# The levels of a blocked triangular inverse: one matrix at a time, or two side by side

## The reference

```python
kb = k * beta[..., None]
lower = jnp.where(strict, jnp.einsum('bnhik,bnhjk->bnhij', kb, k) * decay, 0.0)
tri = lower + jnp.eye(CHUNK, dtype=jnp.float32)
rhs = jnp.concatenate([vb, kb * jnp.exp(g)[..., None]], axis=-1)
sol = lax.linalg.triangular_solve(tri, rhs, left_side=True, lower=True)
...
def step(S, inp):
    u_i, w_i, a_i, qg_i, kt_i, gl_i = inp
    v_new = u_i - jnp.einsum('bhck,bhkv->bhcv', w_i, S)
    o_i = jnp.einsum('bhck,bhkv->bhcv', qg_i, S) + jnp.einsum('bhij,bhjv->bhiv', a_i, v_new)
    S = S * gl_i[..., None, None] + jnp.einsum('bhck,bhcv->bhkv', kt_i, v_new)
```

## Time and profile before

| | |
|---|---|
| median of 3 runs | 1374.46 us (1374.28 to 1375.1) |
| span of the profiled execution | 1372.5 us |
| PE busy | 1327.3 us, 97% of the span |
| weight loads (PEld) busy | 1076.1 us, 78% |
| DVE busy | 972.7 us, 71% |
| ACT busy | 675.3 us, 49% |
| POOL busy | 554.9 us, 40% |
| granted TensorE clock, mean | 0.995 |

### The profile page before, as it was taken

The page is one execution under the profiler, slowest core; times in us unless marked ns, Lnnn a source line. Parts: engine busy times, 40 slices in busy tenths (PEclk is TensorE's granted clock), DMA queues, the critical chain, the costliest instruction groups (busy, mean ns, idle before and its releaser), DMA issues.

```text
span 1372.5 us, 18983 instructions
## 1 busy us (share of the span) xinstructions
PE 1327.3 (97%) x7213; PEld 1076.1 (78%) x7213; DVE 972.7 (71%) x1687; ACT 675.3 (49%) x1018; POOL 554.9 (40%) x372
## 2 busy tenths in 40 slices
PE   7998999999999999999998999999999999998997
PEld 5786888888888888887886678777777878776786
DVE  5587788879787979876337856777767677777413
ACT  6354436363635445364226555556555655655203
POOL 6432334333334333332224785636365563622300
PEclk9999999999999999999999999999999999999999
DMA  7210110111102120206213211112221111119403
GB/s 195 79 36 16 31 47 16 47 47 47 47 17 62 31 62 20 61 22 223 81 43 127 89 31 31 47 47 65 66 55 47 46 47 47 46 46 306 170 1 123
DMA packets 106859, 91.46 MB, mean 67 GB/s; under 512 B 3105, under 2 KB 92306, under 8 KB 106770
## 3 DMA queue, kind: packets, MB, share of 16 engines
q1 hardware_dynamic: 106770, 90.25, 21.7%
HBM read 66.65 MB, written 23.59 MB: 66 GB/s over the span
## 4 chain that ended last, share of the span: by engine, by line
PE 80%; DVE 12%; ACT 4%; issue 3%; DMA 0%; POOL 0%; DVEq 0%; SPq 0%; ACTq 0%
PE psum L518 25%; PE psum L673 17%; PE psum L687 5%; PE psum L2462 4%; PE psum L2436 4%; PE psum L2381 2%; PE psum L2449 2%; DVE terms L1871 2%; PE psum L2369 2%; PE psum L535 2%; PE psum L2347 2%; DVE stick L2019 2%; PE psum L646 2%; PE psum L2322 1%; DVE small_L L1856 1%
## 5 line engine op out<-in xcount | busy, mean ns | idle before, releaser
L518 PE MATMUL psum<-u_hi,w_hi 128*128 128x512 f32 x640 | 260.6, 407 | 3.9 <-DVE u_lo L1583 1.7
L518 PE MATMUL psum<-u_hi,w_lo 128*128 128x512 f32 x640 | 259.0, 405 | 0.0
L518 PE MATMUL psum<-u_lo,w_hi 128*128 128x512 f32 x640 | 258.3, 404 | 0.0
L485 POOL TENSOR_TENSOR w_lo<-w_raw,w_hi 128x1024 fp32r<-128x1024 f32 (+1 forms) x45 | 107.7, 2394 | 251.5 <-ACT w_hi L480 239.2
L518 PEld LDWEIGHTS psum<-u_hi,w_hi 128*128 128x128 f32 x640 | 120.8, 189 | 31.3 <-issue 4.3
L518 PEld LDWEIGHTS psum<-u_hi,w_lo 128*128 128x128 f32 x640 | 120.8, 189 | 25.8 <-issue 1.9
L518 PEld LDWEIGHTS psum<-u_lo,w_hi 128*128 128x128 f32 x640 | 121.1, 189 | 22.1 <-issue 0.5
L1726 DVE SCALAR_TENSOR_TENSOR late<-raw,cols,late 128x1024 f32<-128x1024 f32 x72 | 129.1, 1793 | 1.8
L615 POOL TENSOR_TENSOR w_lo<-w_raw_b,w_hi 128x512 fp32r<-128x512 f32 x40 | 52.7, 1319 | 136.2 <-ACT w_hi L599 136.2
L2019 DVE TENSOR_TENSOR_SCAN stick<-soft 128x1024 f32<-128x1024 f32 (+3 forms) x64 | 103.6, 1618 | 0.2
L480 ACT ACTIVATE w_hi<-w_raw 128x1024 fp32r<-128x1024 f32 (+1 forms) x45 | 45.8, 1019 | 110.1 <-PE psum L518 109.9
(11 more groups left out here) (302 smaller groups left out, 3224.8 us busy)
## 6 DMA issues: line engine op xcount, KB each, us to landing
w_raw<-in_a_w_in SPq DMA_DIRECT2D x33, 512.0 KB, 4.1
w_raw<-in_b_w_in SPq DMA_DIRECT2D x16, 512.0 KB, 5.5
w_raw_b<-in_b_w_in SPq DMA_DIRECT2D x16, 512.0 KB, 5.6
b_rows<-o_part SPq DMA_DIRECT2D x14, 512.0 KB, 3.8
o_rows<-o_part_a SPq DMA_DIRECT2D x12, 512.0 KB, 3.6
x_stage<-in_x SPq DMA_DIRECT2D x8, 512.0 KB, 7.3
out<-fin_o SPq DMA_DIRECT2D x8, 512.0 KB, 2.6
u_lo<-b_rows SPq DMA_DIRECT2D x7, 512.0 KB, 8.2
```

The source lines that it names most:

```text
L485: G.tensor_tensor(lo_tiles(key), raw_tiles(key), hi_tiles(key).bitcast(F32), ALU.subtract).then_inc(lo_done, 1)
L518: mm = PE.matmul(psum[:, half], (w_hi, w_hi, w_lo)[part][:, buffer(key), k], (u_hi, u_lo, u_hi)[part][:, k, half * HALF:(half + 1) * HALF] ...
```

## The change

Two matrices are worked on at once.

- Transposes: two matrices' packed columns (2 x 64) are the weights of one transpose of 128x128. There are 2 a group, 4 a level, in place of 8. Level 3 packs too: ACT copies `invT` into `inv_first` there, and PE's transposes come behind four products of the fill.
- First product: `Lb` holds two matrices' masked columns side by side (`masked`), and the moving side the second columns of both; of the 128x128 result only the two diagonal blocks of 64x64 are wanted. Two matmuls a group in place of four.
- ACT copies these two blocks one by one (each 64 partitions x 2 pairs x 64 columns) into a block-diagonal tile (`crossed`, the half of `inv` that was free), so 4 copies a level where there were 2.
- Second product: weights are the pair's transposes (128x128), the moving side is the block-diagonal tile with 128 columns. Two matmuls a group in place of four.
- POOL fills the block-diagonal tile with zeros once a head, in slot 7, since the tile's place holds other values between heads. ACT waits for it (`cross_zero`) at level 1.
- The order on DVE does not change.

```diff
@@ gpsimd: level_mask, prepare
-                    G.tensor_tensor(packed(Lb[:, g, :, 0:SIDE], l), columns(half_of(dec, g), l, 0),
+                    G.tensor_tensor(packed(masked(g), l), columns(half_of(dec, g), l, 0),
...
+                if s == 7:
+                    qg_done.wait(pool, h, 1)
+                    G.memset(inv[:, :, PAIRS_OF:2 * PAIRS_OF, :], 0.0).then_inc(cross_zero.handle, 1)
@@ scalar: prepare
                     if s == LEVEL_AT[l] - 1:
-                        if l < LEVELS - 1:
-                            for g in range(2):
...
+                        for g in range(2):
+                            if l == 1:
+                                t0_done[g].wait(act, h, 1)
+                            else:
+                                inv_up[g].wait(act, h, l - 1)
+                            A.activation(packed(inv_first[:, g], l), columns(half_of(invT[:, h % 2], g), l, 0),
+                                         ACT.Copy).then_inc(inv_ev[g].handle, 1)
                         for g in range(2):
                             inv_mm[g].wait(act, h, 3 * l - 2)
...
+                            A.activation(turned_pairs(g), turn_bank(g), ACT.Copy).then_inc(inv_ev[g].handle, 1)
                     if s == LEVEL_AT[l]:
                         for g in range(2):
                             inv_mm[g].wait(act, h, 3 * l - 1)
-                            A.activation(Xs[0:SIDE, g, :, 0:SIDE], corners(4 + 2 * g), ACT.Copy
-                                         ).then_inc(inv_ev[g].handle, 1)
+                            if l == 1 and g == 0:
+                                cross_zero.wait(act, h, 1)
+                            for i in range(2):
+                                own = slice(i * SIDE, (i + 1) * SIDE)
+                                A.activation(crossed(g)[own, :, own], product_bank(g)[own, :, own], ACT.Copy
+                                             ).then_inc(inv_ev[g].handle, 1)
@@ tensor: turn, prepare
+                    inv_ev[g].wait(pe, h, packed_ev(l))
+                    for m in range(PAIRS_OF):
+                        first = inv_first[:, g, 2 * m:2 * m + 2, :].rearrange("p i c -> p (i c)")
+                        mm = PE.transpose(turn_bank(g)[:, m], first, ident[:, :])
...
-                if s == LEVEL_AT[LEVELS - 1] - 1:
-                    turn(h, s)
...
-                            for i in range(4):
-                                second = columns(invT[:, c, 4 * g + i:4 * g + i + 1], l, 1)[:, 0]
-                                mm = PE.matmul(corners(4 + 2 * g)[:, i], Lb[:, g, i, 0:SIDE], second,
-                                               start=True, stop=True)
+                            for m in range(PAIRS_OF):
+                                pair = invT[:, c, 4 * g + 2 * m:4 * g + 2 * m + 2]
+                                second = pair.rearrange("p n (b t s) -> p (n b) t s", t=2, s=SMALL << (l - 1))[:, :, 1]
+                                mm = PE.matmul(product_bank(g)[:, m], Lb[:, g, m, :], second, start=True, stop=True)
...
-                            for i in range(4):
-                                rows = changed_rows(l)
-                                mm = PE.matmul(psum[0:rows, 5 + 2 * g, i * SIDE:(i + 1) * SIDE], inv[0:SIDE, g, i, 0:rows],
-                                               Xs[0:SIDE, g, i, 0:SIDE], start=True, stop=True)
+                            for m in range(PAIRS_OF):
+                                mm = PE.matmul(psum[:, 5 + 2 * g, pair_columns(m)], turned_pairs(g)[:, m], crossed(g)[:, m],
+                                               start=True, stop=True)
...
-                    if t + 1 < H and s + 1 in LEVEL_AT[1:LEVELS - 1]:
+                    if t + 1 < H and s + 1 in LEVEL_AT[1:]:
```

## The result

The changed kernel takes 1352.7 us (median of 4 runs, 1351.95 to 1353.51). The kernel before takes 1374.37 beside it (4 runs, 1374.17 to 1375.1). The ratio is 0.9844, with a 95% interval of 0.9832 to 0.9856. The forecast was 1353.0, with 21.5 us gained; 21.7 were. The profiled span fell from 1372.5 to 1351.2.

A forecast was written before the change was run, and what follows sets the result against it. PE bounds layer 0, DVE next. Heads 1 to 6 give 13.8 us, head 7 4.4, head 0 3.3: 21.5 off 1374.46 makes 1353.0 us, range 1339 to 1361.

The forecast's parts named there:

- PE's prices: PE's levels 1 to 3: transposes save 1.19, first products 1.17, second products 2.24, together 4.6 us a head.
- The rule against it: Skill's rule: weight loading costs columns / 1.2 ns whatever the rows; only second products would gain, 0.64 + 0.43 us.
- The rival's 1366: Rival on PE's levels: weight width alone sets the price, about 1 us gained per head, total 1366; chance 0.06.
- DVE's row: DVE's gapless work up to slot 19's `rhs`, slack 0.09: 1.1 us of PE wait, gain there 2.4 instead of 3.5.
- ACT's row: ACT's work from table load to square at head's end, slack 0.1: PE waits, a steady head gains 2.5, not 4.6.
- The fill: POOL's zero fill in each head, possibly holding DVE's chain to the state: 0.2 us, bounds 0 and 0.53.
- The cover of level 3's copies: Four projections ahead of level 3's transposes hide ACT's two new packing copies; without them about 0.7 us.
- The heads: Gains summed by head: heads 1 to 6 13.8 us, head 7 4.4, head 0 3.3 (between 1.5 and 4.6).
- the cover: Rival: DVE's tap starts just ahead of POOL's split, unstretched, `rhs` is early, all heads keep 4.4: 1340; chance 0.16.
- More given back: Rival: fill costs 0.53 a head and narrow slacks leave 2.1 instead of 2.5: 1359.5; chance 0.15.
- The clock: Rival: two new waits in each of heads 1 to 6 lower PE's granted clock; slower, 1381 at 8 us per head; chance 0.05.
- Nothing left: Rival: the work freed on PE is lost to new waits altogether: 1374; chance 0.04.

The follow-up runs named there:

- run 1: Changed kernel, for heads 1 on ACT's load of the Ln and Exp table behind the second square of `o` instead of in front: 1347.18 us.
- run 2: Changed kernel, DVE's lower split of the stored output moved from slot 17 to 18, behind slot 19's `rhs`: 1346.29 us.
- run 3: Changed kernel with both moves: ACT's table load behind the second square of `o`, DVE's lower split behind slot 19's `rhs`: 1340.46 us.
- run 4: Kernel before (no paired levels) with the same two edits, table load behind the square and DVE's lower split behind `rhs`: 1372.95 us, ratio 0.9994.
- run 7: Changed kernel with table load and lower split moved, first products unpaired, all 16 writing partitions 0 to 63 (odd matrices' products left out): 1348.33 us.
- run 9: Changed kernel with table load and lower split moved, second products unpaired: 16 instructions a level, full weights, 64 moving columns each: 1360.35 us.
- Run 5: Changed kernel, POOL's fill with zeros run twice back to back, ACT waiting for the second: 1353.17 us.
- Run 10: Changed kernel with table load and lower split moved, level 3's transposes at the head of their slot's projections, not behind the first four: 1344.95 us.

## Why the prediction held, step by step

The mechanism held: PE's own saving, and the two rows that take part of it back, are as forecast, and runs 1 to 4 show that these two rows do it. That the total is right within 0.3 us is partly luck. In the profiles heads 1 to 6 gained 0.9 more than forecast, and head 0, head 7 and the rest of the program 0.4, 0.25 and 0.5 less.

**PE's prices.** Forecast 4.6 us a head. The pieces of the chain came out as priced (0.44, 0.89, 0.89, no tail). With every new wait gone a round is 76.28 - 71.81 = 4.47 shorter. Undoing the first products alone gives 0.99 for the 1.17 forecast (run 7), so that term was 0.2 too high; the second products and transposes weren't undone in their old form. Against the kernel before with the same two edits it is 4.38.

**The rule against it.** The width of the weights alone should have left the first products and transposes without gain. For work in one half of the partitions it is wrong: run 7 has 1.07 to 1.08 us for 16 instructions of 64 columns, and 8 of 128 take 0.89. It is wrong for the transposes of levels 1 and 2 as well: 8 took 0.87 us with weights of 64 columns and of 128 alike, and 4 take 0.44, so there the count sets the price. With full weights the price is the same for 64 and 128 moving columns (run 9); a projection, which moves 512, takes 0.23. Halves that alternate take 0.61 and with the tail 0.81, less than either. The rival's 1366 is refuted, but the reason in the prediction was incomplete: apart from the tail, the first products were dear because they stood in one half, not because they were narrow.

**DVE's row.** Forecast: 1.1 us of wait at `rhs`. Shown are 0.82, which cost 1.08 (run 2). The size was right as a cost and too large as idle time, since the sum took no account of what a wait costs PE beyond its idle time. In starts of the product the sum had 2.4 us gained with the wait and 3.5 without; measured are 2.44 and 3.41.

**ACT's row.** Here the size is right partly by luck: several terms were off and nearly cancelled. The four block copies took 1.16 us and not 0.94 (0.84 + 0.1): each costs 0.29, so halving the columns saved 0.13 of 0.42 per copy. But they start 2.87 us earlier in the round than the two before (271.43 - 211.69 = 59.74 against 279.63 - 217.02 = 62.61), not 2.7. The table load behind them is then 2.56 us earlier, within the 2.5 to 2.6 forecast. But the prediction got there by taking the slack of 0.1 off, where at DVE's row it had rightly added it; added, it would have made the sum 2.7. And the way from the table load to the square grew, which it didn't foresee: 9.02 us between their starts against 8.87. So the square is ready 2.41 earlier, and PE takes it 2.46 earlier. PE's wait was forecast at 0.8; it shows 0.69 and costs 0.97 (run 1).

**The fill.** Forecast 0.2 a head, bounds 0 and 0.53. Run 5 shows no cost of a second one, and PE's wait for the state is still 0.5 with the first: 7 x 0.2 = 1.4 us too much were put down to it.

**The cover of level 3's copies.** Forecast: about 0.7 without it. Run 10, with both moves in place, has 0.73.

**The heads.** Heads 1 to 6: forecast 13.8, measured 14.7; the difference of 0.9 is the fill's 1.2 less small terms. Head 7: forecast 4.4, measured 4.15; without a cost of the fill it should have been 4.6, and the first products' 0.2 explain less than half of that miss; the rest is open. This round also moves by about 0.25 with the two edits in either kernel: it is 71.44 in run 4 (71.19 without them) and 66.81 in run 3 (67.04), and between these two it is 4.63. Head 0: forecast 3.3, measured 2.92. Here, too, other engines take time back, DVE's split of the squares (`sq_lo_k`) above all. PE's wait for it ahead of the next head's sums grew by 0.8 (first row after, second before), and its waits for ACT's copies to `inv` from 0.3 to 0.7:

```profile
PE psum L2349 <- DVE sq_lo_k L1960: 2.1, 1, 2.1
```

```profile
PE psum L2322 <- DVE sq_lo_k L1927: 1.3, 1, 1.3
```

Its clock differs in both directions. In the changed kernel it stands at 0.50 for the whole of 110 to 116 us (0.73 before), and at 1.00 for 136 to 142 (0.72 before), where the earlier trace rows had its low stretch. What each of these moved was not measured apart. Behind 648 us 0.5 is given back, in small steps between 741 and 1215 us, in layer 1; their cause is open.

**The rivals.** In the kernel as changed the cover did not hold; its time of 1340 is what both moves reach (1340.46), by taking the work from the way and not by a lucky start of the tap. More given back: the fill and the state's wait (still 0.5) speak against it. The clock: it stayed at 1.00 in the steady heads (205 to 577 us) with two more waits in each. Nothing left: refuted by run 4 against run 3 as by the result.

## What to carry to other kernels

Price a shortened engine's gain up to the first point where another engine's row has less slack than the gain, and look for what stands in that row without need: here one table load and one split of 1.22 us held 12 of 34 us. Matrix work of 64 columns should either be paired to full width or be spread over both halves of the partitions it writes; the expensive form is many narrow products in one half. A short wait of TensorE cost 0.26 to 0.28 us more here than its idle time in the profile, so a row that is late by a little is worth moving.

## What the runs showed that was not expected

- 16 matmul instructions of 64 columns of weights and 64 moving columns took 1.07 us with all outputs in partitions 0 to 63, 0.61 with the halves alternating from matrix to matrix, 0.66 with two matrices in one half and then two in the other. The full-width projections behind them took 1.58 to 1.59 in all three, against 1.38 behind full-width work, so the narrow weights ahead of them cost about 0.2 us more, whatever the halves. Behind 16 instructions with full weights and 64 moving columns it was 0.06.
- PE's wait of 0.82, 0.69, 0.49 and 0.45 us cost 1.08, 0.97, 0.76 and 0.73: 0.26 to 0.28 more each time. (The 0.76 was read right behind the wait; a round kept 0.51 of it.)
- POOL's fill of 512 columns (0.52 us) did not slow DVE's two-input operations beside it; POOL's two-input split stretched one of them from about 0.2 to 2.06 us.
- ACT's copies of 64x128 from PSUM took 0.29 us each, those of 64x256 0.42.
